# Whole cache pages in 32 partitions for the top-k attention of a hybrid decoder step

## The chip, the cores and the metric

One core of a Trainium2 chip runs one decoder step. The metric is the device time of one execution in microseconds (us); three executions of the kernel before gave a median of 2479.27 us. The engines are named as the profile names them: PE is TensorE (matmuls and transposes), PEld its weight loads, DVE is VectorE, ACT is ScalarE, POOL is GpSimd, SP is SyncE, which here issues DMAs. SPq and ACTq are those engines' DMA instructions. All DMAs run on the core's 16 DMA engines.

## What is computed

The step takes a prompt of 512 tokens and a batch of 8 samples with 8 new tokens each, and each sample has 4096 past keys in a paged cache (pages of 128 tokens). Three attention mixers run side by side; the change is in mixer B for the samples, `dsa_attention`, where an indexer picks 256 keys per query:

```python
score = jnp.einsum('bqhk,bqh->bqk', jax.nn.relu(s), iw)
vals, idx = lax.top_k(score, top)
k_sel = jax.vmap(lambda a, i: a[i])(k, idx)
v_sel = jax.vmap(lambda a, i: a[i])(v, idx)
logits = jnp.einsum('bqkgd,bqskd->bqkgs', qg, k_sel) * (D_HEAD ** -0.5)
bias = table[t5_bucket(q_pos[None, :, None] - pos_sel)]
p = masked_softmax(logits + bias, valid)
o = jnp.einsum('bqkgs,bqskd->bqkgd', p, v_sel)
```

There are 6 query heads and 2 key/value heads of width 128. The keys and values of one token lie together in `cache_dsa_kv`: key head 0, key head 1, value head 0, value head 1, 4 x 128 floats, which is 2 KB. A page of 128 tokens is 256 KB in one piece of HBM. The softmax and the sum over keys don't depend on the order of the keys, as long as logits, mask, bias and values have the same one.

## The kernel before

The kernel is written engine by engine with semaphores; the order of each engine's work is the order in which its instructions are written. It runs in stages, one after the other: input projection with mixer A beside it, indexer scores, compression, then four sample attentions (`cmp`, `slc`, `dsa`, `win`), then the prompt's attention and the output projection. The change touches the `dsa` stage.

The selection isn't a gather. The kernel reads all 4096 keys of every sample and adds a large negative number to the logits of the keys that weren't picked. The stage is an instance of the function `stream`, which the `slc` and `win` stages use as well. It works on chunks: 4 groups of 2 samples, 8 chunks of 512 keys each, so 32 chunks. A chunk is 4 pages for each of 2 samples, 8 pages or 2.097 MB. Per chunk:

- SP (L899, `load_pages`) issues 8 DMAs, one a page. A page lands with one token in each of the 128 partitions, 2 KB in each. The rows tiles are a ring of 4 chunks (`kept.second`, two halves of `kept.region`, `kept.rows3`, named `kept_second`, `kept_region` and `kept_rows` in the profile); SP waits until the values of the chunk four before are used (`v_used`). The first 3 chunks are issued in the stage before (`step_rows`).
- PE transposes the keys (`turn`, L1628): 4 items (2 samples x 2 key heads), each of 4 transposes of 128x128 into one of two PSUM tiles `tp`.
- ACT copies each item to SBUF (`copy_key`, L1741, `dsa_kT<-dsa_tp`, 128x512). With two `tp` tiles, the transposes of item 2 wait for the copy of item 0, and those of item 3 for the copy of item 1.
- PE adds the mask of keys (L1638) and multiplies keys and queries (`score`, L1641) into `sc`, when all four copies are done.
- DVE (`limit`, L1806) reads `sc`, adds the bias, writes negated logits into `prob` and the running minimum into `nmax`; the profile calls it CUSTOM_DVE_ANT_0.
- ACT (`exps`, L1749 and L1750) makes the exponentials of the chunk before. Its place in ACT's order is between the copies of items 1 and 2.
- PE transposes the probabilities (`turn_probs`, L1651), DVE copies them (`copy_probs`, L1814), PE multiplies with the values (`values`, L1667), DVE adds up (`add_up`, L1824).

In PE's order a chunk is: transposes of four items, transposes of the probabilities of the chunk before, `score`, `values` of the chunk before. ACT's `take_total` (L1459) in the indexer stage is not touched, but is spoken of: it copies 64x512 scores out of PSUM, and writes them as `p (k j) -> p j k` with j of 4, so with 16 bytes from one written element to the next. The load of the 32 partitions of `norm_onehot` (L217) and the loads of 64 partitions of projected rows (`new_rows`, L930) aren't touched either.

Of the kernel before, what the change touches and what calls it, by code (L numbers as in the profile page):

```python
# [20 lines left out]
ALU = mybir.AluOpType  # L21
# [3 lines left out]
P = 128  # L25
# [7 lines left out]
DH = 128  # L33
# [18 lines left out]
PPC = CH // P  # L52
# [843 lines left out]
def load_pages(sp, pages, to, cache, col, width, sem):  # L896
    for p, page in enumerate(pages):
        src = cache[bass.ds(page, 1), :, col:col + width].rearrange("o p c -> (o p) c")
        sp.dma_start(to[:, p], src).then_inc(sem, 16)  # L899
# [2 lines left out]


AHEAD = 3


def step_rows(sp, nc, io, kept, tag, cache, col, n, free):

    g, c = divmod(n, NCH)
    free(n)  # L910
    pages = page_numbers(nc, io, kept.paired, g * (2 * NPG) + c * (2 * PPC), 2 * PPC)
    for b in range(2):
        to = kept.rows[n % 4].rearrange("p (b m c) -> p b m c", b=2, m=PPC)[:, b]
        load_pages(sp, pages[b * PPC:(b + 1) * PPC], to, cache, col, 4 * DH, kept.arrived[tag][n % 4][b])


def new_values(sp, io, kept, tag, col):
# [571 lines left out]


def stream(nc, io, kept, tag, *, cache, col, heads, per, q, k_new, select=None, dropped_keys=None, bias=None,
           bias_in=None, late=None, extra=(), ready=AHEAD, ahead=None, head0, state=None, gate=None, add=False, zero=None, spare=None):


    groups = NB // per
# [5 lines left out]
    width = heads * DH  # L1501
    items = per * heads
# [4 lines left out]
    with ExitStack() as ctx:  # L1507
        s = Scope(nc, ctx, tag)
        rows = [kept.rows[i].rearrange("p (b m c) -> p b m c", b=per, m=PPC) for i in range(SLOTS)]
# [4 lines left out]
        KTS = 8  # L1514
        kT = [s.sb(f"kT{i}", [P, CH]) for i in range(KTS)]

        prob = [s.sb(f"prob{i}", [P, CH]) for i in range(2)]
# [5 lines left out]
        nmax = s.sb("nmax", [P, groups, nch + 1])  # L1523
# [4 lines left out]
        tp = [s.ps(f"tp{i}", [P, CH]) for i in range(2)]  # L1528
        sc = [s.ps(f"sc{i}", [P, CH]) for i in range(2)]
# [4 lines left out]
        rows_in = kept.arrived[tag]  # L1534
        late_in, zeroed = s.sem("late_in"), s.sem("zeroed")
        k_turned, kT_copied, scored = s.sem("k_turned"), s.sem("kT_copied"), s.sem("scored")
# [17 lines left out]
        def parity(g, c):  # L1554
            return c % 2 if nch > 1 else g % 2
# [12 lines left out]
        @block.sync  # L1568
        def _(sp):
            def rows_of(g):  # L1570

                for c in range(nch):
                    n = c + g * nch
                    i, _ = slot(g, c)
                    if state is None and c % 2 == 0 and n + 1 >= ready:

                        pages = page_numbers(nc, io, kept.paired, g * (2 * NPG) + c * (2 * PPC), 4 * PPC)
                    if n < ready:
                        continue
                    for b in range(per):  # L1580

                        sp.wait_ge(v_used, n * per + b + 1)
                        if state is not None:
                            sp.dma_start(rows[i][:, b], state[g * per + b].rearrange("(m p) c -> p m c", p=P)).then_inc(rows_in[i][b], 64)
                        else:
                            first = (c % 2 * per + b) * PPC
                            load_pages(sp, pages[first:first + PPC], rows[i][:, b], cache, col, 2 * width, rows_in[i][b])

            each_group(sp, rows_of)
            for to, first in extra:  # L1590
                sp.wait_ge(zeroed, 3)
                load_bias(sp, io, to, first, KEYS - to.shape[1], later_in)

            def free(n):

                sp.wait_ge(v_used, SLOTS * per + (groups * nch - 4 + n + 1) * per)

            if ahead is not None:
                ahead(sp, free)
# [127 lines left out]
        @block.scalar  # L1727
        def _(act):
            act.preload_act_table_set("natural_log_exp_and_others")
            act.nop().then_inc(kT_copied, 2)  # L1730
            act.nop().then_inc(probs, 2)
            if late is not None:
                act.wait_ge(zeroed, 1)
                load_bias(act, io, late[0], late[2], late[1], late_in)

            def copy_key(g, c, j):
                n = c + g * nch
                act.wait_ge(k_turned, n * items + j + 1 + SLOTS * items)

                act.wait_ge(scored, (n - 1) * items + KTS)  # L1740
                act.copy(kT[(n * items + j) % KTS][:], tp[j % 2][:]).then_inc(kT_copied, 1)  # L1741

            def exps(g, c):

                n = c + g * nch
                act.wait_ge(maxed, n + 2)
                at = parity(g, c)
                one = lambda x, k: x[:, bass.ds(g, 1), k:k + 1].rearrange("p o k -> p (o k)")
                act.activation(prob[at][:], prob[at][:], ACT.Exp, bias=one(nmax, c + 1), scale=-1.0, accum_out=one(sums, c + 1)).then_inc(probs, 1)  # L1749
                act.activation(one(shrink, c + 1), one(nmax, c), ACT.Exp, bias=one(nmax, c + 1), scale=-1.0).then_inc(shrunk, 1)  # L1750

            def group(g):
                for c in range(nch):
                    if before(g, c):
                        for j in range(items):
                            copy_key(g, c, j)
                            if j == 1:
                                exps(*before(g, c))
                if ends(g):
                    exps(g, nch - 1)  # L1760

            for j in range(items):
                copy_key(0, 0, j)
            act.wait_ge(zeroed, 1 + (late is not None))
            act.wait_ge(maxed, 1)
            for g in range(groups):
                act.activation(prob_new[:, g, 0:NT], log_new[:, g, :], ACT.Exp, bias=nmax[:, g, 0:1],
                               accum_out=sums[:, g, 0:1]).then_inc(new_prob, 1)

            each_group(act, group)  # L1770
            for g in range(groups):
                act.activation(share[:, g, :], nmax[:, g, :], ACT.Exp, bias=nmax[:, g, nch:nch + 1], scale=-1.0).then_inc(step_act, 1)

        @block.vector
        def _(dve):
# [17 lines left out]
            def limit(g, c):  # L1793

                n = c + g * nch
                at = parity(g, c)
                here = bias(c * CH, (c + 1) * CH)
                one = lambda x, k: x[:, bass.ds(g, 1), k:k + 1].rearrange("p o k -> p (o k)")
                dve.wait_ge(scored, (n + 1) * items + KTS)

                dve.wait_ge(probs_turned, n + 1)
                dve.wait_ge(maxed, n + 1)
                if late is not None and n * CH == late[1]:
                    dve.wait_ge(late_in, 16 * items)

                dve.tensor_tensor_reduce(prob[at][:], sc[at][:], here, -1.0, one(nmax, c), ALU.add, ALU.min,  # L1806
                                         one(nmax, c + 1)).then_inc(maxed, 1)

            def copy_probs(g, c):
# [54 lines left out]
            each = 3  # L1864
            n = each * NT
            for g in range(groups):
                rows = tp[g // 4][:, g % 4 * P:(g % 4 + 1) * P].rearrange("p (b r) -> p b r", b=per)
                for h in range(heads):
                    got = rows[:, :, h * rise:h * rise + n].rearrange("p b (j t) -> p b j t", t=NT)
                    to = kept.oTs[:, head0 + h * each:head0 + (h + 1) * each, g * per * NT:(g + 1) * per * NT].rearrange("p j (b t) -> p b j t", t=NT)  # L1870
# [10 lines left out]
def dsa_sample(nc, io, kept):  # L1881
    def keys(c):
        return kept.drop[:, PAST:KEYS] if c is None else kept.drop[:, c * CH:(c + 1) * CH]

    def bias(lo, hi):

        if lo >= PAST:
            return kept.bias_lo[:, PAST // 2 + lo - PAST:PAST // 2 + hi - PAST]
        return kept.bias_lo[:, lo:hi] if hi <= PAST // 2 else kept.bias_hi[:, lo - PAST // 2:hi - PAST // 2]

    def ahead(sp, free):
        new_values(sp, io, kept, "win", NSA_VW)
        for g in range(AHEAD):
            free(g)
            for b in range(2):
                to = kept.rows[g].rearrange("p (b m c) -> p b m c", b=2, m=PPC)[:, b]
                sp.dma_start(to, io.win_state[g * 2 + b].rearrange("(m p) c -> p m c", p=P)).then_inc(kept.arrived["win"][g][b], 64)

    stream(nc, io, kept, "dsa", cache=io.dsa_cache, col=0, heads=2, per=2, q=kept.q_dsa, k_new=kept.k_dsa,
           select=kept.sel_d, dropped_keys=keys, bias=bias, bias_in=(kept.bias_lo_in, 128), late=(kept.bias_hi[:], PAST // 2, 0),  # L1900
           extra=((kept.bias_win, 6),), ahead=ahead, head0=4)


def cmp_sample(nc, io, kept):
# [1102 lines left out]
```

## Time and profile before

| | |
|---|---|
| median of 3 executions | 2479.27 us (2478.28 to 2479.59) |
| the profiled execution | 2478.93 us |
| its span, first to last instruction | 2477.2 us |
| PE busy | 2288.4 us, 92% of the span |
| DVE busy | 937.6 us, 38% |
| ACT busy | 857.8 us, 35% |
| POOL busy | 507.6 us, 20% |
| DMA, mean over the span | 211 GB/s |
| `dsa` stage, first PE work to the start of the next stage's | 1766.2 to 1957.3 us |

The shares of the whole span are averages over stages with different limits, so for this change only the stretch of the `dsa` stage counts. The times of the rows further down are microseconds from the span's start. The profiled execution took 1.7 us more than its span, which is what lies around the first and the last instruction.

### The profile page before, as it was taken

The page shows a single profiled execution, that of the slowest core. Times are in us where ns is not written, and L with a number is a line of the kernel's source. Part 1 is how long each engine was busy: PE and PEld are TensorE (multiplying, and loading weights), DVE is VectorE, ACT ScalarE, POOL GpSimd, SP SyncE. Part 2 cuts the span into 40 slices and gives each one's busy share as a digit, 9 for nine tenths or more (in the row PEclk, how much of TensorE's full clock was granted, in tenths as well). Part 3 has the DMA queues.
Part 4 walks back from the last instruction along what each step waited for, and adds up shares of the span by engine and source line. Part 5 has one row for each costly group of instructions (what it writes and reads, how often), then busy time and mean ns, then how long its engine had stood idle before and what let it go on. Part 6 is the DMA issues. An engine that isn't in the chain of part 4 may idle for free. (4 is left out here: it accounts for less than half of the span.)

```text
span 2477.2 us, 46126 instructions
## 1 busy us (share of the span) xinstructions
PE 2288.4 (92%) x16625; PEld 1747.2 (71%) x16625; DVE 937.6 (38%) x1657; ACT 857.8 (35%) x1913; POOL 507.6 (20%) x403
## 2 busy tenths in 40 slices
PE   5999999999999999997899999789799867998996
PEld 3887777767777676774899999555555544777885
DVE  4111121211121111124488886533333347975123
ACT  4000322222222222211444443355455466662010
POOL 6333222222222222221300000000000000445332
PEclk6999999999999999999999999899999876999998
DMA  4755676767667676657666664899999876002323
GB/s 150 209 173 199 230 253 208 263 214 251 236 223 247 229 253 223 205 136 218 188 194 196 194 195 147 249 369 377 319 382 377 294 229 198 1 1 94 120 85 119
DMA packets 322723, 523.15 MB, mean 211 GB/s; under 512 B 36981, under 2 KB 128518, under 8 KB 320662
## 3 DMA queue, kind: packets, MB, share of 16 engines
q1 hardware_dynamic: 302722, 491.76, 59.8%
q10 hardware_dynamic: 16416, 23.13, 2.8%
q0 software_dynamic: 3360, 5.33, 0.6%
q8 instruction: 133, 2.18, 0.4%
q14 instruction: 92, 0.75, 0.1%
HBM read 497.83 MB, written 44.00 MB: 219 GB/s over the span
## 5 line engine op out<-in xcount | busy, mean ns | idle before, releaser
L547 POOL TENSOR_TENSOR proj_w_lo<-kept_region,proj_w_hi 128x1024 fp32r<-128x1024 f32 (+1 forms) x120 | 282.1, 2352 | 743.1 <-DVE proj_w_hi L785 743.1
L565 PE MATMUL proj_acc<-proj_w_hi,h_hi 128*128 128x512 f32 (+1 forms) x960 | 395.0, 411 | 6.0 <-POOL proj_w_lo L547 6.0
L567 PE MATMUL proj_acc<-proj_w_lo,h_hi 128*128 128x512 f32 (+1 forms) x960 | 372.4, 388 | 0.0
L566 PE MATMUL proj_acc<-proj_w_hi,h_lo 128*128 128x512 f32 (+1 forms) x960 | 372.1, 388 | 0.0
L737 ACT COPY proj_kT<-proj_tp 128x512 f32<-128x512 f32 x256 | 150.4, 587 | 406.2 <-PE proj_tp L626 405.9
L565 PEld LDWEIGHTS proj_acc<-proj_w_hi,h_hi 128*128 128x128 f32 x960 | 180.9, 188 | 88.9 <-issue 53.5
L785 DVE CAST proj_w_hi<-kept_region 128x1024 fp32r<-128x1024 f32 (+1 forms) x120 | 86.8, 725 | 400.7 <-PE proj_acc L569 398.1
L567 PEld LDWEIGHTS proj_acc<-proj_w_lo,h_hi 128*128 128x128 f32 x960 | 180.8, 188 | 38.0
L566 PEld LDWEIGHTS proj_acc<-proj_w_hi,h_lo 128*128 128x128 f32 x960 | 181.6, 189 | 27.9
L1191 ACT COPY cmp_xT<-cmp_tp 128x512 f32<-128x512 f32 x260 | 139.3, 588 | 159.1 <-PE cmp_tp L1104 159.0
L626 PE MATMUL proj_tp<-kept_consts,kept_region 128*128 128x128 f32 x1024 | 153.6, 272 | 0.2 <-DMA kept_region<-in_cache_sb_kv_dram 0.2
L626 PEld LDWEIGHTS proj_tp<-kept_consts,kept_region 128*128 128x128 f32 x1024 | 126.4, 140 | 35.6 <-ACT proj_kT L737 4.9
L1104 PE MATMUL cmp_tp<-kept_consts,kept_second 128*128 128x128 f32 x1040 | 138.2, 277 | 6.3 <-DMA kept_second<-in_cache_nsa_kv_dram 5.4
L963 DVE MAX8 kept_top<-kept_scores 64x8 f32<-64x4104 f32 x32 | 141.5, 4423 | 0.5
L965 DVE MATCH_REPLACE8 kept_scores<-kept_top,kept_scores 64x4104 f32<-64x4104 f32 x32 | 141.1, 4409 | 0.0
L1104 PEld LDWEIGHTS cmp_tp<-kept_consts,kept_second 128*128 128x128 f32 x1040 | 119.8, 143 | 8.5 <-DMA kept_second<-in_cache_nsa_kv_dram 6.8
L1162 PE MATMUL cmp_hp<-cmp_xT,kept_region 128*128 128x128 f32 x1024 | 125.5, 276 | 0.0
L1162 PE MATMUL cmp_hp<-cmp_xT,kept_w_values 128*128 128x128 f32 x1024 | 123.8, 275 | 0.0
L1162 PEld LDWEIGHTS cmp_hp<-cmp_xT,kept_region 128*128 128x128 f32 x1024 | 120.1, 193 | 0.0
L1162 PEld LDWEIGHTS cmp_hp<-cmp_xT,kept_w_values 128*128 128x128 f32 x1024 | 118.9, 192 | 0.0
L693 ACT COPY proj_out<-proj_acc 128x512 f32<-128x512 f32 (+1 forms) x60 | 34.6, 578 | 218.3 <-PE proj_acc L567 218.3
L2784 PE MATMUL fin_acc<-fin_w_hi,fin_o_hi 128*128 128x512 f32 x256 | 100.6, 393 | 7.9 <-DVE fin_o_lo L2842 6.4
(446 smaller groups left out, 3607.0 us busy)
## 6 DMA issues: line engine op xcount, KB each, us to landing
kept_region<-in_cache_sb_kv_dram SPq DMA_DIRECT2D x256, 256.0 KB, 4.9
kept_second<-in_cache_sb_kv_dram SPq DMA_DIRECT2D x256, 256.0 KB
kept_second<-in_cache_nsa_kv_dram SPq DMA_DIRECT2D x512, 128.0 KB, 2.4
kept_region<-in_w_in_dram SPq DMA_DIRECT2D x112, 512.0 KB, 5.8
kept_region<-in_cache_nsa_kv_dram SPq DMA_DIRECT2D x128, 256.0 KB, 5.0
kept_region<-in_cache_dsa_kv_dram SPq DMA_DIRECT2D x128, 256.0 KB, 4.8
kept_second<-in_cache_nsa_kv_dram SPq DMA_DIRECT2D x64, 256.0 KB, 4.8
kept_rows<-in_cache_nsa_kv_dram SPq DMA_DIRECT2D x64, 256.0 KB, 5.5
```

The costliest lines, as they stand in the source:

```text
L547: pool.tensor_tensor(w_lo[p % SPLIT][:, :, here], w[p % RAW][:, :, here], w_hi[p % SPLIT][:, :, here], ALU.subtract).then_inc(lo_made, 1)
L565: pe.matmul(to, h_hi[:, kk, r], hi[:, k], start=first, stop=False)
L566: pe.matmul(to, h_lo[:, kk, r], hi[:, k], start=False, stop=False)
L567: last = pe.matmul(to, h_hi[:, kk, r], lo[:, k], start=False, stop=final)
L626: last = pe.transpose(tp[:, x:x + P], k_rows[:, b, p, h * DH:(h + 1) * DH], kept.ident)
L737: act.copy(kT[:, h % 2, 2 * pair:2 * pair + 2, :], tp[:].rearrange("p (b k) -> p b k", b=2)).then_inc(kT_copied, 1)
L963: dve.max(kept.top8[:], kept.scores[:]).then_inc(kept.top_step, 1)
L965: dve.match_replace(kept.scores[:], kept.top8[:], kept.scores[:], GONE).then_inc(kept.top_step, 1)
L1104: last = pe.transpose(tp[n % 2 * 2 + a][:, p * P:(p + 1) * P], rows[i][:, p, a, :], kept.ident)
L1162: last = pe.matmul(hp[e][:, a, :], w1(2 * e + a, r), xT[:, 2 * e + a, r, :], start=(r == 0), stop=(r == CMPB - 1))
L1191: act.copy(xT[:, a, :, to], tp[n % 2 * 2 + own][:].rearrange("p (c r) -> p r c", r=CMPB)).then_inc(x_copied, 1)
L2784: pe.matmul(to[:], o_hi[:, h, r], hi[:, k, :], start=first, stop=False)
```

## The change

The page lands otherwise. A new function loads a page into 32 partitions, tokens 4t to 4t+3 of the page into partition t of the page's quarter, 8 KB in one piece. The four pages of a sample go to the four quarters of the partitions, and are issued in the order 0, 2, 1, 3. The bytes, the number of DMAs, the tiles and every wait stay. `slc` and `win` keep the old form.

After that, slice m of the rows tile holds in partition x the token 4x + m of the chunk, where it held token x of page m. So two operations put the order right. The copy of the keys writes column (m, x) of `tp` to column 4x + m of `kT`; logits, mask and bias then stand in the natural order. The write of `limit` goes the other way: logit 4x + m to column (m, x) of `prob`, so that each 128x128 transpose of the probabilities fits the values' partitions.

```diff
+KPP = 4
+PAGE_ORDER = (0, 2, 1, 3)
+
+
+def load_whole_pages(sp, pages, to, cache, sem):
+
+    each = P // KPP
+    for p in PAGE_ORDER:
+        src = cache[bass.ds(pages[p], 1), :, :].rearrange("o (t j) c -> (o t) (j c)", j=KPP)
+        sp.dma_start(to[p * each:(p + 1) * each].rearrange("t j c -> t (j c)"), src).then_inc(sem, 16)
...
-        load_pages(sp, pages[b * PPC:(b + 1) * PPC], to, cache, col, 4 * DH, kept.arrived[tag][n % 4][b])
+        if tag == "dsa":
+            load_whole_pages(sp, pages[b * PPC:(b + 1) * PPC], to, cache, kept.arrived[tag][n % 4][b])
+        else:
+            load_pages(sp, pages[b * PPC:(b + 1) * PPC], to, cache, col, 4 * DH, kept.arrived[tag][n % 4][b])
...
-                act.copy(kT[(n * items + j) % KTS][:], tp[j % 2][:]).then_inc(kT_copied, 1)
+                to, src = kT[(n * items + j) % KTS][:], tp[j % 2][:]
+                if whole:
+                    to, src = to.rearrange("d (x j) -> d j x", j=KPP), src.rearrange("d (j x) -> d j x", j=KPP)
+                act.copy(to, src).then_inc(kT_copied, 1)
...
-                dve.tensor_tensor_reduce(prob[at][:], sc[at][:], here, -1.0, one(nmax, c), ALU.add, ALU.min,
+                to, logits = prob[at][:], sc[at][:]
+                if whole:
+                    to = to.rearrange("r (j x) -> r x j", j=KPP)
+                    logits, here = (v.rearrange("r (x j) -> r x j", j=KPP) for v in (logits, here))
+                dve.tensor_tensor_reduce(to, logits, here, -1.0, one(nmax, c), ALU.add, ALU.min,
                                          one(nmax, c + 1)).then_inc(maxed, 1)
```

In `stream` the loads of the later chunks switch in the same way under `whole`, which only the `dsa` stage sets. No instruction is added, taken away or moved on any engine; three kinds change their form. The key copies go from 128x512 to 128x4x128, the page loads from 128x512 to 32x2048, and `limit` from 128x512 to 128x128x4.

## Rows read from the trace of the kernel before

**Rows 1.** Stretches of the stage: length, busy (instructions) per engine, clock, DMA share, GB/s.
```profile
1850.00:1900.00 50.00, 45.81 (x551) 29.55 (x551) 16.18 (x36) 26.46 (x64) 0.00 (x0) 1.00 1.04 378
```

**Rows 2.** Waits, 1765 to 1960 us: who, for whom, us in total, times, longest.
```profile
ACT dsa_kT L1741 <- PE dsa_tp L1628: 85.7, 35, 3.2
...
PE dsa_tp L1628 <- ACT dsa_kT L1741: 7.7, 32, 0.3
...
PE dsa_sc L1641 <- ACT dsa_kT L1741: 5.6, 32, 0.3
...
PE dsa_tp L1628 <- DMA kept_rows<-in_cache_dsa_kv_dram: 0.6, 1, 0.6
```

**Rows 3.** Timeline of one chunk: start, us, engine, line, operation, count [idle before].
```profile
1842.49 0.08 DVE L1806 DVE_READ_ACCUMULATOR2_ANT dsa_nmax<- 128x1 f32 x1
...
1842.55 1.09 PE L1628 MATMUL dsa_tp<-kept_consts,kept_region 128*128 128x128 f32 x8
...
1843.24 1.07 ACT L1741 COPY dsa_kT<-dsa_tp 128x512 f32<-128x512 f32 x2 [2.62 <-PE dsa_tp L1628]
...
1843.88 1.14 PE L1628 MATMUL dsa_tp<-kept_consts,kept_region 128*128 128x128 f32 x8 [0.24 <-ACT dsa_kT L1741]
1844.20 0.73 ACT L1749 ACTIVATE dsa_prob<-dsa_prob,dsa_nmax 128x512 f32<-128x512 f32 x1
...
1845.11 1.07 ACT L1741 COPY dsa_kT<-dsa_tp 128x512 f32<-128x512 f32 x2
...
1846.23 1.06 PE L1641 MATMUL dsa_sc<-dsa_kT,kept_q_dsa 128*32 128x512 f32 x8 [0.17 <-ACT dsa_kT L1741]
...
1847.11 1.06 PE L1667 MATMUL dsa_pv<-kept_second,dsa_pT 128*32 128x128 f32 x32
...
1848.10 0.33 PE L1628 MATMUL dsa_tp<-kept_consts,kept_region 128*128 128x128 f32 x1
```

**Rows 4.** Groups of ACT copies: busy us, mean ns | idle before.
```profile
L1741 ACT COPY dsa_kT<-dsa_tp 128x512 f32<-128x512 f32 x128 | 68.8, 590 | 85.7 <-PE dsa_tp L1628 85.7
...
L1459 ACT COPY kept_scores<-idx_total 64x512 f32<-64x512 f32 x8 | 8.6, 1105 | 46.3 <-issue 24.6 <-PE idx_total L1393 21.7
...
L695 ACT COPY proj_low<-proj_acc 64x512 f32<-64x512 f32 x14 | 8.2, 586 | 7.2 <-PE proj_acc L569 7.2
```

**Rows 5.** The group of `limit` on DVE, first half of the keys, columns as in rows 4.
```profile
L1806 DVE CUSTOM_DVE_ANT_0 dsa_prob<-dsa_sc,kept_bias_lo,dsa_nmax 128x512 f32<-128x512 f32 x16 | 12.0, 750 | 18.8 <-PE dsa_sc L1641 18.8
```

**Rows 6.** Stretches of DMA into 32, 128 and 64 partitions, columns as in rows 1.
```profile
11.50:14.00 2.50, 2.50 (x14) 2.50 (x12) 0.15 (x1) 2.10 (x3) 0.95 (x8) 1.00 0.89 188
...
15.00:18.00 3.00, 1.58 (x10) 1.32 (x11) 3.00 (x5) 1.70 (x3) 2.08 (x5) 0.90 1.01 415
1091.00:1093.50 2.50, 2.50 (x18) 2.48 (x18) 0.00 (x0) 1.03 (x3) 0.00 (x0) 1.00 0.96 225
1092.00:1093.00 1.00, 1.00 (x8) 1.00 (x7) 0.00 (x0) 0.50 (x2) 0.00 (x0) 1.00 1.10 248
```

**Rows 7.** SP's DMA issues at the start and before 1093 us, columns as in rows 3.
```profile
2.15 0.51 SPq L217 DMA_DIRECT2D norm_onehot<-in_onehot_dram  x1
...
1089.72 2.42 SPq L930 DMA_DIRECT2D kept_region<-proj  x4
```

**Rows 8.** SP's issues of `dsa` pages at the stage's border, columns as in rows 3.
```profile
1747.84 4.65 SPq L899 DMA_DIRECT2D kept_second<-in_cache_dsa_kv_dram  x8
1753.23 11.19 SPq L899 DMA_DIRECT2D kept_region<-in_cache_dsa_kv_dram  x16
```

**Rows 9.** Timeline where the last chunk's second sample is waited for.
```profile
1943.62 0.86 PEld L1628 LDWEIGHTS dsa_tp<-kept_consts,kept_rows 128*128 128x128 f32 x8 [0.81 <-DMA kept_rows<-in_cache_dsa_kv_dram]
```

**Rows 10.** The first `win` chunk, with the clock at its lower level, columns as in rows 1.
```profile
1958.00:1966.00 8.00, 6.71 (x28) 3.92 (x28) 1.61 (x5) 3.49 (x12) 0.00 (x0) 0.50 0.81 291
```

**Rows 11.** Loads of indexer pages into 32 partitions, from SP: ns min/median/max of the issue.
```profile
L952 SPq DMA_DIRECT2D idx_rows<-in_cache_dsa_idx_dram x64: 315/316/1310, 1099.6 to 1136.3; - x64
```

More of the change, by code:

```diff
@@ L1491, in stream @@
 def stream(nc, io, kept, tag, *, cache, col, heads, per, q, k_new, select=None, dropped_keys=None, bias=None,
-           bias_in=None, late=None, extra=(), ready=AHEAD, ahead=None, head0, state=None, gate=None, add=False, zero=None, spare=None):
+           bias_in=None, late=None, extra=(), ready=AHEAD, ahead=None, head0, state=None, gate=None, add=False, zero=None, spare=None, whole=False):
     groups = NB // per
@@ L1586, in rows_of @@
                             first = (c % 2 * per + b) * PPC
-                            load_pages(sp, pages[first:first + PPC], rows[i][:, b], cache, col, 2 * width, rows_in[i][b])
+                            if whole:
+                                load_whole_pages(sp, pages[first:first + PPC], rows[i][:, b], cache, rows_in[i][b])
+                            else:
+                                load_pages(sp, pages[first:first + PPC], rows[i][:, b], cache, col, 2 * width, rows_in[i][b])
             each_group(sp, rows_of)
@@ L1804, in limit @@
                     dve.wait_ge(late_in, 16 * items)
-                dve.tensor_tensor_reduce(prob[at][:], sc[at][:], here, -1.0, one(nmax, c), ALU.add, ALU.min,
+                to, logits = prob[at][:], sc[at][:]
+                if whole:
+                    to = to.rearrange("r (j x) -> r x j", j=KPP)
+                    logits, here = (v.rearrange("r (x j) -> r x j", j=KPP) for v in (logits, here))
+                dve.tensor_tensor_reduce(to, logits, here, -1.0, one(nmax, c), ALU.add, ALU.min,
                                          one(nmax, c + 1)).then_inc(maxed, 1)
@@ L1900, in dsa_sample @@
            select=kept.sel_d, dropped_keys=keys, bias=bias, bias_in=(kept.bias_lo_in, 128), late=(kept.bias_hi[:], PAST // 2, 0),
-           extra=((kept.bias_win, 6),), ahead=ahead, head0=4)
+           extra=((kept.bias_win, 6),), ahead=ahead, head0=4, whole=True)
 def cmp_sample(nc, io, kept):
```

## The prediction

> **What bounds the kernel now.** The stretches of the stage come first [rows 1]. In 50 us in the middle of it PE is busy 45.8 us at the full clock, DVE 16.2 us and ACT 26.5 us, and the DMA engines have a share of 1.04 and move 378 GB/s. The reader is to see two things close to their limit at once, PE and DMA. The waits tell which ends last [rows 2]. PE waits for ACT's key copies in each of the 32 chunks (7.7 us before the transposes, 5.6 us before `score`), and for rows from a DMA once in the stage, 0.6 us. So PE and ACT's copies set the pace, and the transfers just keep up.
>
> The timeline of one chunk shows the chain [rows 3]. The transposes start at 1842.55, the first copy at 1843.24, the exponentials after two copies at 1844.20, the third copy at 1845.11, `score` at 1846.23, and the next chunk's transposes at 1848.10. A period is 5.55 us. From 1843.24 on ACT works through without a gap: two copies, exponentials, two copies. The transposes of items 2 and 3 wait 0.24 us for a copy, `score` 0.17 us for the last one. ACT's 2.94 us from the first copy's start to the last one's end are on the path, with no slack at all.
>
> The transfers' slack follows from the same period: 2.097 MB in 5.55 us needs 378 GB/s. The last chunk's second sample was already waited for until 1943.62 [rows 9].
>
> **The key copies.** The change gives 128 copies a write with 16 bytes from one element to the next. The trace has the same form on the same engine: `take_total`, 64x4x128, written with 16 bytes between elements, reads PSUM in order as the new copy does. It takes 1105 ns [rows 4]. The same engine's copy of 64x512 in order takes 586 ns, and the key copy 590 ns. So neither the number of partitions nor the source explains the difference, and the write's step is what is left. I take 1105 - 590 = 515 ns more for each copy. The lower bound is 0, if something else in the indexer stage slows that copy; a gain is excluded, as there are as many elements as before.
>
> All four copies of a chunk lie on the path. In the new chunk the first copy starts 0.69 us after the transposes, the exponentials 0.96 + 1.03 = 1.99 us later, the third copy 0.91 us after that, `score` 1.12 + 1.03 = 2.15 us after that, and the next chunk 1.87 us after `score`: 0.69 + 1.99 + 0.91 + 2.15 + 1.87 = 7.61 us, against 5.55. That is 2.06 us a chunk and 65.9 us for 32.
>
> **The write of `limit`.** It takes 750 ns now [rows 5]. Nothing in the rows shows DVE writing in steps of 512 bytes. Not below 750 ns, since the elements are the same; above, I take the ratio of the copies, 1105/590, which makes 1.40 us. In the chunk shown it ends at 1842.57 and the exponentials, which wait for it, start at 1844.20: 1.63 us of cover, and 1.03 us more with the slower copies ahead of them [rows 3]. DVE is busy a third of the time. It costs 0 under either end. If the cover were gone, each 0.1 us would cost 3.2 us.
>
> **The page loads.** There are as many DMAs, so SP issues as often. Eight pages take SP 4.65 us now [rows 8]; an indexer page into 32 partitions takes it 316 ns [rows 11], so 2.5 us for eight would be the new price. SP's issuing isn't waited for, so this is worth 0.
>
> What matters is how fast a page lands in 32 partitions. The trace has one such load with enough bytes, `norm_onehot`, 529 KB into 32 partitions, issued at 2.15 us behind two tiles of the prompt [rows 7]. While it lands, from 11.5 to 14 us, the core moves 188 GB/s at a DMA share of 0.89; from 15 to 18 us, with 8 KB rows into 128 partitions, it is 415 GB/s [rows 6]. The second case is the loads of L930 into 64 partitions, issued at 1089.72 [rows 7]: 225 GB/s over 2.5 us at a share of 0.96, with 248 GB/s in its best microsecond [rows 6]. So the engines are as busy as ever, and move about half. Large packets don't help where few partitions are written.
>
> Each of the new loads has such a target, and they go out in one queue after each other. The order 0, 2, 1, 3 puts neighbouring loads in different halves of the partitions. No row shows whether two such loads overlap. The ends are 188 GB/s, not at all, and 415 GB/s, fully. I take 225 GB/s, the steadiest of the rows for few partitions: each DMA engine works through its queue in order, so all of them are mostly at the same page.
>
> The Trainium skill, SBUF — State Buffer, in "Door 1: The DMA port swizzle", says that a range of partitions inside 0 to 63 reaches half of the 16 ports, for which it gives 218 GB/s at best, and under "Can I just issue two DMAs to hit both halves?" that two concurrent DMAs at partitions 0 and 64 gained 6% over one. The trace agrees on the half (188 to 248 against 415 GB/s), and doesn't show the second. By 218 GB/s the estimate would be 9.6 us a chunk and 2594 us.
>
> At 225 GB/s a chunk takes 2.097/0.225 = 9.32 us, more than the 7.61 us of the copies, so the loads set the pace and the copies hide behind them. SP starts with the stage's pages at 1747.84 [rows 8]. Thirty-two chunks without a gap end at 1747.84 + 298.2 = 2046.1, where the last one ended at 1943.62 before [rows 9]: 102.5 us later. Behind the last landing stand four slower copies (2.06 us) and the first item, whose transposes used to lie ahead (they started 1.2 us before): 105.8 us.
>
> **The sum.** The profiled execution took 2478.93 us, 1.7 us more than its span and 0.3 us less than the median. 2478.9 + 105.8 = 2584.7, so 2585 us. The stages behind are shifted and keep their length.
>
> **Rivals.**
>
> *The copies set the pace.* If the two halves overlap so that more than 2.097/7.61 = 276 GB/s come in, the stage goes at 7.61 us a chunk: 2478.9 + 65.9 = 2545 us. For it: the order of the pages, and three chunks of rows in flight, which let an engine run ahead of its neighbour. Against it: it needs 23% more than 225 GB/s, and all loads share one queue.
>
> *The clock falls.* With loads setting the pace PE idles about half of each period. If it then gets the lower of its two clocks, 1.2 GHz, as in the first `win` chunk at a granted clock of 0.50 [rows 10], the 0.69 us before the first copy and the 1.87 us from `score` on double: 7.61 + 2.56 = 10.2 us a chunk, (10.2 - 5.55) x 32 = 149 us, 2628 us.
>
> *No change.* The copies of 16-byte steps cost what others cost, since the 1105 ns belong to the indexer stage, and the halves overlap fully. Both must hold. The point from which it decides is sharp: 39 ns more on each of 128 copies are 5 us, 0.2% of the time, and any rate under 378 GB/s makes PE wait. At 415 GB/s a chunk lands in 5.05 us, hidden under 5.55; the one wait for rows, 0.6 us, goes, which gives 2478 us. More could only come from waits at the stage's start, a few us. The eight copies of 1105 ns and the two stretches at half the rate speak against it.
>
> *Only the loads are slow.* If the copies cost nothing extra but the rate is 225 GB/s, the result is 2.1 us less than the forecast, and can't be told from it by the time; the mean of the copies tells.
>
> **How the numbers follow.** Loads set the pace: 0.62. Its ends are 248 GB/s (8.46 us a chunk, 1747.8 + 270.6 = 2018.4, 78 us more, 2557 us) and 188 GB/s (11.15 us, 2104.8, 164 us more, 2643 us). Copies set the pace: 0.24, at 2545 us. Clock: 0.06, at 2628 us. No change: 0.08, of which 0.03 faster by a little more than 0.2%. The range of 2540 to 2645 us takes in the first three and leaves some 0.15 out. A measurement of this kernel can tell about 0.2%, 5 us, from no change. Slower by more than that: 0.92; within it: 0.05; faster: 0.03.
>
> **What would show it.** The mean of the key copies near 1.1 us, with the waits of PE for them grown from 13 us, shows the first step. A stretch in mid-stage with about 225 GB/s at a DMA share near 1 shows the second, and so do waits of PE for the DMA of the cache in nearly every chunk. A period of 7.6 us without waits for DMAs is the first rival. A granted clock of 0.5 inside the stage is the second. `limit` above 2.6 us would break the step that hides it. Key copies near 590 ns together with 378 GB/s would make the whole prediction wrong.

## The result: 88 us slower

The changed kernel takes 2566.94 us in the median of five executions (2544.34 to 2572.72), the one before 2479.27 us in the same runs. The ratio is 1.034, with a 95% interval from 1.030 to 1.038. The forecast was 2585 us, in a range of 2540 to 2645 us. The profiled execution of the changed kernel took 2544.34 us (span 2542.6 us), the fastest of the five, so its rows show 65 us of the 88. The kernel's own scatter has grown from 3 us to 28 us; that is part of the result and is taken up below.

The stretches of the stage, in the columns of [rows 1] (length, PE, PEld, DVE, ACT, POOL, clock, DMA share, GB/s):

```profile
1790.00:1850.00 60.00, 43.40 (x488) 26.90 (x488) 16.41 (x32) 36.70 (x57) 0.00 (x0) 0.97 1.02 280
1850.00:1900.00 50.00, 35.96 (x414) 22.38 (x414) 13.66 (x27) 29.37 (x44) 0.00 (x0) 0.97 1.02 270
1900.00:1950.00 50.00, 35.95 (x376) 22.22 (x377) 12.34 (x24) 30.12 (x48) 0.00 (x0) 0.93 1.03 261
```

The DMA engines have the same share as in [rows 1], 1.02 to 1.03, but move 261 to 280 GB/s instead of 378. ACT is busier, PE less. The waits from 1765 to 2035 us, which answer to [rows 2]:

```profile
PEld dsa_sc L1657 <- ACT dsa_kT L1760: 41.0, 32, 1.4
PEld dsa_tp L1644 <- ACT dsa_kT L1760: 39.8, 57, 1.4
PE dsa_sc L1657 <- ACT dsa_kT L1760: 30.7, 32, 1.1
PE dsa_tp L1644 <- ACT dsa_kT L1760: 25.9, 53, 1.0
...
PE dsa_tp L1644 <- DMA kept_region<-in_cache_dsa_kv_dram: 4.8, 5, 1.9
PE dsa_tp L1644 <- DMA kept_rows<-in_cache_dsa_kv_dram: 4.3, 3, 2.6
...
PE dsa_tp L1644 <- DMA kept_second<-in_cache_dsa_kv_dram: 2.9, 3, 1.6
```

PE waited 13.3 us for the key copies before; now it is 56.6 us. For the cache's DMAs it waited 0.6 us; now it is 12.0 us, in 11 places. In this execution the copies come last more often than the loads: 18 of the 31 periods of the stage, from one `score` to the next, are the copies' own (7.35 us or less), and the others are longer, up to 10.1 us.

The groups of the copies and of `limit`, which answer to [rows 4] and [rows 5], with the indexer's copy that I took the price from:

```profile
L1760 ACT COPY dsa_kT<-dsa_tp 128x512 f32<-128x512 f32 x128 | 127.5, 1082 | 99.1 <-PE dsa_tp L1644 99.0
...
L1829 DVE CUSTOM_DVE_ANT_0 dsa_prob<-dsa_sc,kept_bias_lo,dsa_nmax 128x512 f32<-128x512 f32 x16 | 18.4, 1148 | 34.5 <-PE dsa_sc L1657 34.5
...
L1472 ACT COPY kept_scores<-idx_total 64x512 f32<-64x512 f32 x8 | 8.6, 1100 | 46.7 <-issue 25.0 <-PE idx_total L1406 21.7
```

A key copy went from 590 to 1082 ns, `limit` from 750 to 1148 ns. One chunk, in which no load is waited for, answers to [rows 3]:

```profile
1845.23 1.09 PE L1644 MATMUL dsa_tp<-kept_consts,kept_region 128*128 128x128 f32 x8
...
1845.92 1.97 ACT L1760 COPY dsa_kT<-dsa_tp 128x512 f32<-128x512 f32 x2 [2.61 <-PE dsa_tp L1644]
...
1847.69 0.71 ACT L1768 ACTIVATE dsa_prob<-dsa_prob,dsa_nmax 128x512 f32<-128x512 f32 x1
...
1848.57 1.96 ACT L1760 COPY dsa_kT<-dsa_tp 128x512 f32<-128x512 f32 x2
...
1850.59 1.07 PE L1657 MATMUL dsa_sc<-dsa_kT,kept_q_dsa 128*32 128x512 f32 x8 [1.07 <-ACT dsa_kT L1760]
...
1852.46 0.99 PE L1644 MATMUL dsa_tp<-kept_consts,kept_rows 128*128 128x128 f32 x7
```

The period is 7.23 us instead of 5.55. The two pairs of copies take 1.97 and 1.96 us where they took 1.07 each. `score` used to wait 0.17 us for the last copy and now waits 1.07 us.

### The profile page after: what moved, and what is told of

It is laid out like the page before. It is cut to its first block and busy times, and to the rows that moved or that the text cites. A ratio compares the mean times of both kernels' runs of the same rounds, so it can differ in the third digit from the quotient of the medians.

```text
span 2542.6 us, 46123 instructions
## 1 busy us (share of the span) xinstructions
PE 2300.4 (90%) x16622; PEld 1752.3 (69%) x16625; DVE 946.0 (37%) x1657; ACT 912.1 (36%) x1913; POOL 505.9 (20%) x403
## 5 line engine op out<-in xcount | busy, mean ns | idle before, releaser
L1760 ACT COPY dsa_kT<-dsa_tp 128x512 f32<-128x512 f32 x128 | 127.5, 1082 | 99.1 <-PE dsa_tp L1644 99.0
```

Source lines behind the costliest of these rows:

```text
L1760: act.copy(to, src).then_inc(kT_copied, 1)
```

## The experiments

Each group of kernels was timed beside the kernel before on the same chip, at 2476.5 to 2477.3 us there; differences are against that. Where only a part of the change is in, keys, masks and values don't belong together and the numbers computed are others; the work stays the same.

### The copies alone

```diff
-        if tag == "dsa":
+        if False:
             load_whole_pages(
...
-                            if whole:
+                            if False:
                                 load_whole_pages(
...
-                if whole:
-                    to = to.rearrange("r (j x) -> r x j", j=KPP)
-                    logits, here = (v.rearrange("r (x j) -> r x j", j=KPP) for v in (logits, here))
```

> Page loads as before (128 partitions) and limit as before; only the key copies keep the write with 16 bytes between elements, so keys and masks don't belong together. Theory 1, copies and loads each set a floor and the later one paces: the four copies alone lengthen a chunk from 5.55 to about 7.2 us, 53 us in all, 2532 us, with almost no wait for DMAs. Theory 2, the loads set the pace of the changed kernel and the copies hide behind them: the same 2532 here, since nothing hides them now. A theory that the copies cost nothing: 2479.

Measured: 2531.1 us, 53.8 us more, ratio 1.022 (1.020 to 1.024). A key copy takes 1086 ns and a period is 7.24 us. The DMA engines are no limit here, at a share of 0.86 to 0.89:

```profile
1790.00:1850.00 60.00, 42.77 (x497) 1.00 0.88 290
1850.00:1900.00 50.00, 36.62 (x420) 0.97 0.86 285
```

(Columns here and in the stretches further down: length, PE busy, clock, DMA share, GB/s.) So the copies are a floor of their own, 54 us above the kernel before.

### The write of `limit` alone

```diff
-                if whole:
-                    to, src = to.rearrange("d (x j) -> d j x", j=KPP), src.rearrange("d (j x) -> d j x", j=KPP)
```

(with the loads of before again, as above)

> Only the write of limit in steps of 512 bytes, loads and key copies as before, so probabilities and values don't belong together. It took 1.15 us in the changed kernel against 0.75 before, and ends 1.6 us ahead of the exponentials. Hidden: within 1 us of 2479. If it were on the path: 32 x 0.4 = 13 us, 2492.

Measured: 2480.33 us, ratio 1.0008 (0.9998 to 1.0018), no difference that this measurement can tell. `limit` took 1138 ns:

```profile
L1827 DVE CUSTOM_DVE_ANT_0 dsa_prob<-dsa_sc,bias_hi,dsa_nmax 128x512 f32<-128x512 f32 x16 | 18.2, 1138 | 14.3 <-PE dsa_sc L1657 14.3
```

It is slower by half, and hidden.

### The loads alone

```diff
-                if whole:
-                    to, src = to.rearrange("d (x j) -> d j x", j=KPP), src.rearrange("d (j x) -> d j x", j=KPP)
...
-                if whole:
-                    to = to.rearrange("r (j x) -> r x j", j=KPP)
-                    logits, here = (v.rearrange("r (x j) -> r x j", j=KPP) for v in (logits, here))
```

> Only the page loads into 32 partitions, key copies and limit as before (keys and masks don't belong together). Theory 1: the halves overlap in part, 250 to 310 GB/s as in the changed kernel's trace, mean about 265, 7.9 us a chunk, 2536 us, and the rate wanders within the trace. Theory 2 as predicted: 225 GB/s, 9.3 us a chunk, 2583 us, the same as the changed kernel or more. If the loads cost nothing: 2479. Copies and loads as additive costs would make copies_only and loads_only sum to the changed kernel's 88 us.

Measured: 2563.31 us, 86.0 us more, ratio 1.035 (1.033 to 1.036). Neither theory had the number: I wrote 2536 us for 265 GB/s and 2583 us for 225 GB/s. The rate is in between:

```profile
1790.00:1850.00 60.00, 40.58 (x399) 0.89 1.02 243
1850.00:1900.00 50.00, 33.29 (x360) 0.90 1.03 246
1900.00:1950.00 50.00, 34.26 (x359) 0.89 1.03 243
1950.00:2000.00 50.00, 37.23 (x370) 0.86 1.02 254
```

and PE waits for the cache's loads in almost every chunk, 69.4 us in 29 places:

```profile
PE dsa_tp L1644 <- DMA kept_region<-in_cache_dsa_kv_dram: 35.6, 15, 3.3
...
PE dsa_tp L1644 <- DMA kept_rows<-in_cache_dsa_kv_dram: 18.0, 7, 3.4
...
PE dsa_tp L1644 <- DMA kept_second<-in_cache_dsa_kv_dram: 15.8, 7, 3.6
```

Copies alone cost 54 us and loads alone 86 us; both together cost 93 us in the same group of runs (next). They are two floors, and the higher one nearly alone decides. That is the shape that the prediction gave them.

### The changed kernel again

> The changed kernel once more, for a second trace. The first one took 2544 us while the median was 2567. Theory 1: this one is nearer the median, with the key copies' mean and period floor the same (7.2 us) and a lower DMA rate over the stage, about 250 GB/s instead of 270. If the difference came from the clock: the same rate, and a granted clock of 0.5 in several stretches of the stage.

Measured: 2569.87 us, 92.6 us more, ratio 1.039 (1.037 to 1.040), its profiled execution 2562.42 us. The key copies are as before (1085 ns). The stage's rate is 233 GB/s to 1850 us and then climbs:

```profile
1790.00:1850.00 60.00, 44.27 (x444) 0.89 1.03 233
1850.00:1900.00 50.00, 35.78 (x356) 0.84 1.03 240
1900.00:1950.00 50.00, 36.35 (x374) 0.92 1.03 270
1950.00:2000.00 50.00, 36.70 (x418) 0.97 1.02 291
```

At 291 GB/s the loads have reached the copies' floor: 2.097 MB in 7.23 us are 290 GB/s. From 1790 to 2000 us the mean is 257 GB/s here and 273 GB/s in the first trace, and this execution was 18 us longer. The stage has to move the same bytes in both, so a lower mean rate says that the stage was longer, and not yet why. The whole stage with the same 2032 PE instructions, in the copies-alone kernel, in the changed kernel's first trace and in this one:

```profile
1762.00:2015.50 253.50, 179.96 (x2032) 0.95 0.86 284
...
1762.00:2024.20 262.20, 186.42 (x2032) 0.92 1.02 272
...
1762.00:2036.50 274.50, 199.20 (x2032) 0.87 1.00 262
```

Between the two traces of the changed kernel the stage grew by 12.3 us. PE was busy 12.8 us longer for the same work at the lower clock, waited 2.6 us more for loads (14.6 us in 13 places) and 5.3 us less for copies (51.3 us). So the difference reaches the time mainly as slower matmuls, and the granted clock, which I had set as the mark of another cause, has a share in it. Two of its low stretches follow waits for a load (two lines of the timeline, then the stretches):

```profile
1817.97 1.09 PE L1644 MATMUL dsa_tp<-kept_consts,kept_region 128*128 128x128 f32 x8 [1.41 <-DMA kept_region<-in_cache_dsa_kv_dram]
...
1835.85 1.25 PE L1644 MATMUL dsa_tp<-kept_consts,kept_second 128*128 128x128 f32 x8 [1.76 <-DMA kept_second<-in_cache_dsa_kv_dram]
...
1822.00:1828.00 6.00, 5.35 (x50) 0.63 1.02 234
1838.00:1846.00 8.00, 7.35 (x61) 0.66 1.02 235
```

Whether the late loads bring the low clock about isn't shown: the copies-alone kernel, without late loads, has two periods of 8.9 us too. No run held the clock or the rate fixed.

### Two neighbours in the same half

```diff
-PAGE_ORDER = (0, 2, 1, 3)
+PAGE_ORDER = (0, 1, 2, 3)
```

(on top of the loads alone)

> As loads_only (key copies and limit as before, so the key order is wrong), but the pages of a sample are issued in the order 0, 1, 2, 3, so that two loads in a row write the same half of the partitions. loads_only had 243 to 268 GB/s and 2563 us. If the alternation of halves gives some overlap: less rate, down to 218 to 230 GB/s, 9.1 to 9.6 us a chunk, 2578 to 2595 us. If the rate is a property of 32-partition loads alone and the order does nothing: 2563.

Measured: 2589.49 us, 112.8 us more, ratio 1.043 (1.038 to 1.048), and 229 GB/s from 1790 to 2020 us, against 248 GB/s with the order of the change:

```profile
1790.00:1850.00 60.00, 40.72 (x418) 0.87 1.02 222
1850.00:1900.00 50.00, 33.40 (x306) 0.80 1.02 225
```

The order of pages in the change is worth some 27 us of loads. One of four executions took 2567 us, so this layout scatters too, and that one execution lies near those of the order 0, 2, 1, 3.

### 64 partitions instead of 32

```diff
-    each = P // KPP
-    for p in PAGE_ORDER:
-        src = cache[bass.ds(pages[p], 1), :, :].rearrange("o (t j) c -> (o t) (j c)", j=KPP)
-        sp.dma_start(to[p * each:(p + 1) * each].rearrange("t j c -> t (j c)"), src).then_inc(sem, 16)
+    for p in range(4):
+        half, pair = p % 2, p // 2
+        src = cache[bass.ds(pages[p], 1), :, :].rearrange("o (t j) c -> (o t) (j c)", j=2)
+        to_here = to[half * 64:(half + 1) * 64, 2 * pair:2 * pair + 2].rearrange("t j c -> t (j c)")
+        sp.dma_start(to_here, src).then_inc(sem, 16)
```

> As loads_only, but a page lands in 64 partitions, 4 KB in each (two tokens in a row), in the lower and the upper 64 partitions by turns; the key order is wrong. If what counts is the half of the partitions that a load reaches: the same as loads_only, 243 to 268 GB/s, 2555 to 2570 us. If the rate goes with the number of partitions: twice the rate, PE sets the pace again, 2478 to 2485 us.

Measured: 2566.82 us, 90.2 us more, ratio 1.036 (1.033 to 1.039); 252 GB/s from 1790 to 2020 us, 248 GB/s with 32 partitions. Twice the partitions and half the packet's size change nothing. The Trainium skill says so in SBUF — State Buffer, "Door 1: The DMA port swizzle": 0 to 63 reach no more ports than 0 to 31.

### 64 partitions across the middle

```diff
+        if lay == 0:
+            sp.dma_start(to[32:96, m].rearrange("t j c -> t (j c)"), src).then_inc(sem, 16)
+        else:
+            sp.dma_start(to[0:32, m].rearrange("t j c -> t (j c)"), src[0:32]).then_inc(sem, 16)
+            sp.dma_start(to[96:128, m].rearrange("t j c -> t (j c)"), src[32:64]).then_inc(sem, 16)
...
-                    pe.wait_ge(rows_in[i][b], filled * 64)
+                    pe.wait_ge(rows_in[i][b], filled * (96 if whole else 64))
```

> As loads_64 (64 partitions, 4 KB in each, key order wrong), but pages 0 and 1 of a sample land in partitions 32 to 95, and pages 2 and 3 in two loads each, partitions 0 to 31 and 96 to 127. If what counts is on which side of partition 64 a load lies, the first two reach both sides and go at the full rate: 1.05 MB at 415 GB/s and 1.05 MB at 225 to 245 GB/s are 6.8 to 7.2 us a chunk, about 300 GB/s, 2519 to 2532 us. If any load into 64 partitions is slow: as loads_64, 2567 us, or more, as there are 12 loads a chunk instead of 8.

Measured: 2566.44 us, 89.9 us more, ratio 1.038 (1.034 to 1.041). The time that I gave for my theory, 2519 to 2532 us, was wrong; by the time alone it would fall. Microseconds show more. Three pairs of neighbouring ones in this kernel:

```profile
1853.00:1854.00 1.00, 0.52 (x5) 1.00 1.08 315
1854.00:1855.00 1.00, 0.76 (x8) 1.00 1.07 238
1857.00:1858.00 1.00, 1.00 (x26) 1.00 1.06 324
1858.00:1859.00 1.00, 1.00 (x28) 1.00 1.06 229
1861.00:1862.00 1.00, 0.00 (x0) 1.00 0.95 328
1862.00:1863.00 1.00, 0.86 (x6) 0.77 0.98 197
```

and two of the same microseconds with each load on one side of partition 64:

```profile
1853.00:1854.00 1.00, 0.01 (x1) 1.00 1.04 246
...
1857.00:1858.00 1.00, 1.00 (x6) 0.50 1.06 250
```

The rate goes up and down, about once in the time of a sample's pages, between some 200 and some 330 GB/s, where the kernel with one-sided loads stays near 250. That fits loads across the middle running well above 250 GB/s for a moment. But the mean from 1790 to 2020 us is 255 GB/s, against 252 GB/s with one-sided loads into 64 partitions, so nothing is won over the stage. Why not, with half of the bytes in loads across the middle, is open; there are 12 loads a chunk instead of 8. Which microsecond belongs to which load isn't in these rows, so this supports the reading and doesn't prove it.

### One queue for each half

```diff
+            def odd_half(n):
+                if not ready <= n < groups * nch:
+                    return
+                g, c = divmod(n, nch)
+                i, _ = slot(g, c)
+                pages = page_numbers(nc, io, kept.paired, g * (2 * NPG) + c * (2 * PPC), 2 * PPC, mybir.EngineType.Activation)
+                act.wait_ge(v_used, (n + 1) * per)
+                for b in range(per):
+                    load_whole_pages(act, pages[b * PPC:(b + 1) * PPC], rows[i][:, b], cache, rows_in[i][b], (2, 3))
```

(called by ACT behind a chunk's last key copy for the chunk two ahead; SP issues pages 0 and 1)

> As loads_only, but from the fourth chunk on the pages of the upper 64 partitions (2 and 3) are issued by ACT behind its last key copy of a chunk, those of the lower 64 by SP; the key order is wrong. Each DMA engine then has two queues and takes from both, so both halves are written at the same time. If the engines' order within one queue keeps one half idle (theory 1): the rate rises to what PE asks for, 350 to 378 GB/s, 2480 to 2495 us. If a 32-partition load is slow by itself: 2563 as before, with the waits for DMAs unchanged.

> The whole change with the loads on two queues, as in two_queues_loads. Theory 1: only the key copies are left as a cost, 2531 us as copies_only, a few us more if ACT's issuing comes in the way of its copies. If the loads stay slow: 2560 to 2575 us as the changed kernel.

Measured: 2593.24 us for the loads alone (ratio 1.046, 1.044 to 1.048) and 2598.74 us for the whole change (1.047, 1.042 to 1.051). Both are slower than with one queue, by 30 and 29 us, and the rate is the lowest of all:

```profile
1790.00:1850.00 60.00, 37.98 (x371) 0.84 1.01 216
1850.00:1900.00 50.00, 36.53 (x351) 0.80 1.03 220
```

So the idea that the order within one queue keeps one half idle, and that a second queue would cure it, falls in this form. The test changes one thing more: ACT asks for its half of a chunk 5.9 to 8.0 us after SP (four chunks from 1840 to 1880 us), so less is queued ahead. The DMA share stays at 1.01 to 1.03, and no run with two queues had both halves asked for at the same time.

### The same copy, read with steps and written in order

```diff
-                    to, src = to.rearrange("d (x j) -> d j x", j=KPP), src.rearrange("d (j x) -> d j x", j=KPP)
+                    src = src.rearrange("d (j x) -> d x j", j=KPP)
+                    to = to.rearrange("d (x j) -> d x j", j=KPP)
```

> As copies_only (page loads as before, key order wrong), with the same elements moved in the other order: the key copy writes SBUF in order and reads PSUM with 512 bytes between elements, four at a time. If the cost is in the write of single elements 16 bytes apart: 590 ns a copy and 2479 us. If any order that isn't contiguous costs: about 1085 ns and 2531 us as copies_only. If long steps in PSUM cost more than short ones in SBUF: above 1085 ns and above 2531 us.

> The whole change, with the key copy that reads with steps and writes in order. If the read is free: the loads alone are left, 2563 us as loads_only. If it costs as the write: 2567 to 2570 us as the changed kernel.

The first has the loads of before, the second is the whole change. Measured: 2475.38 us, ratio 0.9996 (0.9986 to 1.0006), the same as before, and a key copy takes 590 ns:

```profile
L1761 ACT COPY dsa_kT<-dsa_tp 128x512 f32<-128x512 f32 x128 | 68.6, 590 | 84.9 <-PE dsa_tp L1644 84.9
```

Every element goes to the same place as in the copies-alone kernel; only the order in which ACT walks over them differs. The cost was the write of single elements 16 bytes apart. Reading PSUM with 512 bytes between elements costs nothing.

The whole change with this copy took 2516.65, 2549.37, 2556.62 and 2567.69 us. They are too far apart for an interval, but the fastest is 35 us above the slowest of the kernel before beside it (2481.77). The median is 2552.99 us, 76.5 us more. What is left is the loads: in the profiled execution PE waited 53.1 us for the cache's DMAs and 9.2 us for the copies. No kernel tried is faster than the one before by more than the scatter.

## Why the prediction was right, and where it was off

**What bounds the kernel before.** Right. ACT's copies lie on the path without slack: making only them slower cost 53.8 us. The loads just keep up: making only them slower cost 86.0 us.

**The copies.** The price was good, 515 ns more forecast and 492 ns measured, and the reason was right, as the write's step is the whole of it. The sum over a chunk was too high, 2.06 us against 1.68 us (7.23 - 5.55), so 65.9 us against 53.8 us for the copies alone. I added 1.03 us for each pair of copies. The time from the first copy to the exponentials grew by 0.81 us (from 0.96 to 1.77), that from the third copy to `score` by 0.90 us (from 1.12 to 2.02), and the gap from the exponentials' start to the third copy shrank from 0.91 to 0.88 us: 1.68 us together.

**`limit`.** Right. It got slower by 0.40 us, within the bound of 0.65 us, and costs nothing. One sign was put wrongly: the 2.66 us of cover come on top of the 0.75 us that `limit` takes, so it would have had to exceed 3.4 us, not 2.6. Nothing hangs on it.

**The loads.** The step is right: loads into 32 partitions, or into 64 on one side of partition 64, move at a little over half of the 415 GB/s of [rows 6], at a DMA share of 1.02. That the side counts, and not only a span under 128 partitions, rests on the order of pages (248 against 229 GB/s) and on single microseconds of the loads across the middle, whose mean didn't rise. The size was off. I took 225 GB/s, from loads that stood alone; the loads-alone kernel had 243 to 254 GB/s in mid-stage and the changed kernel 233 to 291. The alternating order gives an overlap of the halves, which I had left to the rival: 248 against 229 GB/s in the mean. This is the mis-sized term. By its own sum 248 GB/s, my upper end, gave 78 us, and 225 gave 106 us; 88 us were measured.

A second term was off the other way. The sum lets the pages land without a gap from 1747.84 us on, and at 248 GB/s the last one would be there at 2018.4 us. In the loads-alone kernel, with 247 GB/s from 1790 us on, PE waited for it until 2032.37 us, 14 us later:

```profile
2032.37 1.09 PE L1644 MATMUL dsa_tp<-kept_consts,kept_rows 128*128 128x128 f32 x8 [3.44 <-DMA kept_rows<-in_cache_dsa_kv_dram]
```

What I left out stands in the trace of before. SP's queue already held a `slc` chunk and the bias lines, issued 4 to 9 us ahead of the first `dsa` page:

```profile
1739.03 4.51 SPq L899 DMA_DIRECT2D kept_rows<-in_cache_nsa_kv_dram  x8
1743.59 3.24 SPq L998 DMA_DIRECT2D kept_bias_lo<-token_lines  x8
```

How much of the 14 us they account for wasn't tested. So the rate made the forecast 28 us too long and the start some 14 us too short. That 106 came as near to 88 as it did is partly luck.

**The copies hide behind the loads.** Half right. The experiments say that the loads are the higher floor: 86 us alone, 76.5 us with the copy that costs nothing, against 54 us for the copies. But in the changed kernel PE waited for loads in 11 and 13 places, not in nearly every chunk, and 18 and 13 of 31 periods were the copies' 7.23 us. Against the kernel before, the stage of the second trace is 81.5 us longer: 38.0 us more of waits for copies, 14.0 us more of waits for loads, and 29.5 us more of busy PE for the same 2032 instructions (169.69 us before). Of these, 10.3 us are there in the copies-alone kernel too; the other 19.2 us came with the lower clock. The late loads show more in longer periods than in waits put down to them.

**SP's issuing.** I gave 2.5 us for eight pages. They took 3.8 us in most chunks of the changed kernel and up to 5.0 us, still hidden.

**The sentence why 225.** Its reason was that all DMA engines are mostly at the same page. The measured effect of the order fits mostly, not always; no row shows which page an engine is at. The two queues don't fit it in any simple form, since pages of both halves were queued at once there and the rate fell.

**Half of the ports.** The runs gave 216 to 291 GB/s for one-sided loads. The Trainium skill's 218 GB/s (SBUF — State Buffer, "Door 1: The DMA port swizzle") was below what alternating loads got, and just met by the two queues (216 to 231). Its 6% for two loads in opposite halves would give, as an estimate, 231 GB/s; the order 0, 2, 1, 3 had 243 to 254 in the loads-alone kernel, and 8% over the order 0, 1, 2, 3.

**The rivals.** *The copies set the pace* is the case for stretches, whenever the rate reaches 290 GB/s, and for more than half of the periods of the first trace. So the two cases that I had set apart take turns within one execution. *The clock falls* came in part, and for more than I gave it: the granted clock was 0.84 to 0.92 from 1790 to 1950 us of the second trace, so the lower level in a minority of the time, and PE was busy 19.2 us longer over the stage than in the copies-alone kernel (199.20 against 179.96 us). *No change* fell on both of its conditions.

**What stays open.** Why the rate of the same loads wanders between 233 and 316 GB/s. The rows don't show at which page each DMA engine is, and no run here set it. How much of the scatter is the loads and how much the clock is open, and so is why two queues are worse.

## What to carry to other kernels

Before a load is cut into fewer partitions with longer rows, compare bytes and not packets: here 8 KB rows into 32 partitions came in at 216 to 291 GB/s over 50 us and more, 2 KB rows into 128 partitions at 378. Where a copy has to change an order, let it read with steps and write in order; the same permutation cost 492 ns a copy the one way and nothing the other. Two costs that each set a floor for the same loop don't add up (54 and 86 us gave 93), so each has to be measured alone before one is repaired.

## What the runs showed of the hardware

- The rate of one-sided loads isn't a constant. In the changed kernel's first trace it was 316 GB/s from 1830 to 1840 us and 256 GB/s from 1900 to 1910 us, with the same instructions:

```profile
1830.00:1840.00 10.00, 7.25 (x103) 1.00 1.02 316
...
1900.00:1910.00 10.00, 7.51 (x74) 1.00 1.03 256
```

- ACT's write of single fp32 elements 16 bytes apart takes 1.8 to 1.9 times the time of a write in order, in 64 partitions (1100 against 586 ns) as in 128 (1082 against 590 ns). The same permutation read from PSUM in steps of 512 bytes and written in order takes 590 ns. DVE's write in steps of 512 bytes takes 1.5 times (1138 against 750 ns).
- The DMA share doesn't tell a transfer at half rate from one at full rate. It is 1.02 at 243 GB/s and 1.04 at 378 GB/s.
- Sending the two halves of the partitions through two queues on the same DMA engines lowered the rate from 248 to 223 GB/s, with one half asked for 5.9 to 8.0 us later.
